# The last stage of a hybrid encoder block: the final norm's weights applied before the norm's power is known

## What is computed

```
u = causal_depthwise_conv(h @ w_up, ffn_conv_w) + ffn_conv_b
gate, val = jnp.split(u, 2, axis=-1)
y = (gelu(gate) * val) @ w_down
return x + rms_norm(y, g_post_ffn)     # y * rsqrt(mean(y*y) + EPS) * g_post_ffn
```

## Time and profile before

| | us |
|---|---|
| median of 3 runs | 1303.62 (1303.28 to 1305.38) |
| the profiled execution's own time | 1303.67 |
| its span in the profile | 1301.4 |
| TensorE (PE) busy | 1255.1 (96%) |
| VectorE (DVE) busy | 696.9 (54%) |
| ScalarE (ACT) busy | 410.7 (32%) |
| GpSimd (POOL) busy | 148.3 (11%) |

### The profile page before, as it was taken

The page is one execution under the profiler, slowest core; times in us unless marked ns, Lnnn a source line. Parts: engine busy times, 40 slices in busy tenths (PEclk is TensorE's granted clock), DMA queues, the critical chain, the costliest instruction groups (busy, mean ns, idle before and its releaser), DMA issues.

```text
span 1301.4 us, 17346 instructions
## 1 busy us (share of the span) xinstructions
PE 1255.1 (96%) x6360; PEld 1062.5 (82%) x6360; DVE 696.9 (54%) x1069; ACT 410.7 (32%) x754; POOL 148.3 (11%) x183
## 2 busy tenths in 40 slices
PE   6999999997999999899999999999999999999997
PEld 5888888876888889778888888888888888888875
DVE  6332454657767777563563636363636363535366
ACT  5121243645444444353312121212121212121321
POOL 1321001302322232121000000000000000000005
PEclk9999999997999999999999999999999999999999
DMA  8321233564233331232211111111111111110133
GB/s 275 123 80 54 81 103 103 150 190 121 73 110 109 108 108 45 92 106 81 78 52 46 50 44 53 41 55 39 58 36 60 34 62 34 62 34 30 37 125 129
DMA packets 90762, 106.52 MB, mean 82 GB/s; under 512 B 17471, under 2 KB 75615, under 8 KB 90719
## 3 DMA queue, kind: packets, MB, share of 16 engines
q1 hardware_dynamic: 90719, 105.96, 25.2%
HBM read 82.84 MB, written 23.10 MB: 81 GB/s over the span
## 4 chain that ended last, share of the span: by engine, by line
PE 53%; POOL 1%; issue 1%; DVE 0%; ACT 0%; POOLq 0%; DVEq 0%
PE f_ps_up L2383 12%; PE f_ps_up L2385 12%; PE f_ps_up L2384 12%; PE sums L2394 5%; PE sums L2395 5%; PE sums L2396 5%; POOL stage L2101 1%; POOL f_conv L2101 0%; POOL f_stat L2367 0%; POOLq L2006 0%; DVE split L2336 0%; DVE h_t L2301 0%; DVE f_conv L2101 0%; ACT x_tile L2233 0%; DVE h_t L2259 0%
## 5 line engine op out<-in xcount | busy, mean ns | idle before, releaser
L2383 PE MATMUL f_ps_up<-split,f_w_hi 128*128 128x512 f32 x704 | 274.3, 390 | 1.7 <-DVEq L2237 1.5
L2385 PE MATMUL f_ps_up<-split,f_w_lo 128*128 128x512 f32 x704 | 273.9, 389 | 0.0
L2384 PE MATMUL f_ps_up<-split,f_w_hi 128*128 128x512 f32 x704 | 273.9, 389 | 0.0
L2247 DVE SCALAR_TENSOR_TENSOR f_conv<-f_ps_up,f_taps,f_conv 128x1023 f32<-128x1023 f32 x88 | 112.8, 1282 | 272.3 <-ACT f_conv L2176 266.8
L2383 PEld LDWEIGHTS f_ps_up<-split,f_w_hi 128*128 128x128 f32 x704 | 132.1, 188 | 29.9 <-DVEq L2237 1.9
L2385 PEld LDWEIGHTS f_ps_up<-split,f_w_lo 128*128 128x128 f32 x704 | 132.1, 188 | 27.5
L2176 ACT ACTIVATE f_conv<-f_ps_up,f_taps 128x1024 f32<-128x1024 f32 x44 | 53.1, 1207 | 321.4 <-PE f_ps_up L2385 321.4
L2384 PEld LDWEIGHTS f_ps_up<-split,f_w_hi 128*128 128x128 f32 x704 | 132.2, 188 | 27.3
L2259 DVE TENSOR_TENSOR h_t<-sums,h_t 128x512 f32<-128x512 f32 x168 | 111.0, 685 | 39.9 <-PE sums L2396 39.7
L2394 PE MATMUL sums<-f_w_hi,f_y_hi 128*128 128x512 f32 x320 | 124.6, 389 | 0.0
L2396 PE MATMUL sums<-f_w_hi,y_lo 128*128 128x512 f32 x320 | 124.5, 389 | 0.0
(11 more groups left out here) (320 smaller groups left out, 2058.8 us busy)
## 6 DMA issues: line engine op xcount, KB each, us to landing
stage<-in_w_up SPq DMA_DIRECT2D x22, 1024.0 KB, 5.1
stage<-in_w_down SPq DMA_DIRECT2D x11, 1024.0 KB, 4.9
x_tile<-in_x SPq DMA_DIRECT2D x12, 512.0 KB, 4.0
stage<-in_w_in SPq DMA_DIRECT2D x6, 1024.0 KB, 6.7
qkv<-conv SPq DMA_DIRECT2D x11, 512.0 KB, 3.6
rows<-p_row SPq DMA_DIRECT2D x8, 644.0 KB, 3.2
stage<-rows SPq DMA_DIRECT2D x8, 644.0 KB, 4.0
res<-x_tile SPq DMA_DIRECT2D x8, 512.0 KB, 2.9
```

The source lines that it names most:

```text
L2247: op = dve.scalar_tensor_tensor(conv[:, q, k:S], ps_up[:, q % 2, 0:S - k], taps[:, bass.ds(ct + (FTAPS - 1 - k) * 2 * FT, 1)], conv[:, q, ...
L2383: pe.matmul(bank, hi, h_hi[:, k, cols], start=(k == ends[0]), stop=False)
L2384: pe.matmul(bank, hi, h_lo[:, k, cols], start=False, stop=False)
L2385: op = pe.matmul(bank, lo, h_hi[:, k, cols], start=False, stop=(k == ends[1]))
```

## The change

Four edits, all in the last stage.

- The square of a row tile is made in two halves of 512 columns, each as soon as its half is accumulated; the two sums go to two columns of `f_stat`.
- The mean is made in two steps on VectorE: `mean` takes the first half's sum, `mean_late` adds the second half's.
- The weights are multiplied in by two operations of 128 x 512, from `acc` into a separate tile `scaled` that lies where `raw_rest` and the start of `split` lie, before the power is known. `finish` then is one operation over 128 x 1024, on VectorE: `scaled` by the row's number, plus the residual.
- GpSimd makes the powers only. VectorE's order for a row tile now is: accumulate the first half, scale it, `mean`; accumulate the second half, scale it, `mean_late`, `finish` of the same row tile; then the next row tile.

```diff
-            eng.tensor_tensor(res_tile(t), res_tile(t), acc[:, t], ALU.add).then_inc(s_res, 1)
+        self.late = under("late", [P, D])
+        scaled = kept.late
@@ scalar
-                act.wait_ge(s_acc, LAST_SUM + 2 * t + 2 + 4)
-                act.activation(junk[:], acc[:, t], ACT.Square, accum_out=stat[:, 0, t:t + 1]).then_inc(s_sq, 1)
+                for half in range(2):
+                    cols = slice(half * HALF, (half + 1) * HALF)
+                    act.wait_ge(s_acc, LAST_SUM + 2 * t + half + 1 + 4)
+                    act.activation(junk[:, cols], acc[:, t, cols], ACT.Square, accum_out=stat[:, SUMS + half, t:t + 1]).then_inc(s_sq, 1)
@@ vector
+            def scale(t, half):
+                cols = slice(half * HALF, (half + 1) * HALF)
+                dve.wait_ge(s_acc, LAST_SUM + 2 * t + half + 1 + 4)
+                if t >= 1:
+                    dve.wait_ge(s_res, t)
+                dve.tensor_tensor(scaled[:, cols], acc[:, t, cols], gain[:, cols], ALU.mult).then_inc(s_norm, 1)
+            def mean(t):
+                dve.wait_ge(s_sq, 2 * t + 1)
+                dve.tensor_scalar(stat[:, MEAN, t:t + 1], stat[:, SUMS, t:t + 1], 1.0 / D, EPS, ALU.mult, ALU.add).then_inc(s_ms, 1)
+            def mean_late(t):
+                dve.wait_ge(s_sq, 2 * t + 2)
+                dve.wait_ge(s_ms, 2 * t + 1)
+                dve.scalar_tensor_tensor(stat[:, MEAN, t:t + 1], stat[:, SUM_LATE, t:t + 1], 1.0 / D, stat[:, MEAN, t:t + 1],
+                                         ALU.mult, ALU.add).then_inc(s_ms, 1)
             def finish(t):
-                if t == T - 1:
-                    residual(dve, t - 1)
                 dve.wait_ge(s_rstd, t + 1)
-                dve.scalar_tensor_tensor(acc[:, t], acc[:, t], stat[:, 2, t:t + 1], gain[:], ALU.mult, ALU.mult).then_inc(s_norm, 1)
-                if t == T - 1:
-                    residual(dve, t)
+                dve.wait_ge(s_norm, 2 * t + 2)
+                dve.wait_ge(s_xr[t // 4], 64)
+                dve.scalar_tensor_tensor(res_tile(t), scaled[:], stat[:, RSTD, t:t + 1], res_tile(t), ALU.mult, ALU.add).then_inc(s_res, 1)
-            for t in range(T + 1):
-                if t < T:
-                    for half in range(2):
-                        accumulate(LAST_SUM + 2 * t + half, t, half)
-                if t >= 1:
-                    finish(t - 1)
-                if t < T:
-                    dve.wait_ge(s_sq, t + 1)
-                    dve.tensor_scalar(stat[:, 1, t:t + 1], stat[:, 0, t:t + 1], 1.0 / D, EPS, ALU.mult, ALU.add).then_inc(s_ms, 1)
+            for t in range(T):
+                accumulate(LAST_SUM + 2 * t, t, 0)
+                scale(t, 0)
+                mean(t)
+                accumulate(LAST_SUM + 2 * t + 1, t, 1)
+                scale(t, 1)
+                mean_late(t)
+                finish(t)
@@ gpsimd
-                pool.wait_ge(s_ms, t + 1)
-                pool.tensor_tensor(stat[:, 2, t:t + 1], stat[:, 1, t:t + 1], power[:], ALU.pow).then_inc(s_rstd, 1)
-                if 1 <= t < T - 1:
-                    residual(pool, t - 1)
+                pool.wait_ge(s_ms, 2 * t + 2)
+                pool.tensor_tensor(stat[:, RSTD, t:t + 1], stat[:, MEAN, t:t + 1], power[:], ALU.pow).then_inc(s_rstd, 1)
```

More of the change, by code:

```diff
@@ L2025, in ffn_block @@
         taps = sb("f_taps", [P, NT + 2 * FT])
-        stat = sb("f_stat", [P, 3, T])
+        stat = sb("f_stat", [P, 5, T])
         power = sb("f_power", [P, 1])
@@ L2094, in res_tile @@
             return raw[:, 1 - t // 2, t % 2 * D:(t % 2 + 1) * D] if t < 4 else conv[:, t - 4]
[L2096 to L2100, removed]
-            eng.tensor_tensor(res_tile(t), res_tile(t), acc[:, t], ALU.add).then_inc(s_res, 1)
+        SUMS, SUM_LATE, MEAN, RSTD = 0, 1, 2, 3
+        scaled = kept.late
         @block.sync
```

## The result

| | before | after |
|---|---|---|
| median in us (22 runs each, taken side by side) | 1304.45 | 1306.39 |
| the profiled execution's own time | 1303.67 | 1306.49 |
| its span | 1301.4 | 1304.7 |
| first accumulation of the last stage to VectorE's last end ("the stretch") | 1260.96 to 1298.39: 37.43 | 1261.32 to 1301.67: 40.35 |

The ratio of the times, after over before, is 1.0015, 95% interval 1.0009 to 1.0022: 1.9 us slower, between 1.2 and 2.9. A second series (11 runs of the changed kernel, in the experiments) gives 1.0024, 1.0012 to 1.0036. Slower is settled; on which side of 0.2% it lies isn't. The stretch is the better ruler, since it holds all that the change touches: 2.92 us longer.

What follows compares the result with a forecast made beforehand. TensorE was taken to set the pace, with a 6.22 us tail behind it. Changed, eight VectorE turns of 5.07 us plus 0.08 end at 1301.60, not 1298.39: 1303.67 + 3.2 = 1306.9 us, range 1305.0 to 1309.0.

Steps and rivals of the forecast that it cites:

- late mean behind the first accumulation's start: In VectorE's turn: `mean_late` starts 3.03 us after the turn's first accumulation starts, behind the second half's square.
- finish, likewise: In VectorE's turn: `finish` starts 3.87 us after the first accumulation starts, after a stall on GpSimd's power.
- a turn: VectorE's sequence for one row tile, first accumulation to the next tile's: 5.07 us, run eight times.
- tail from the last accumulation: After the last sum: accumulation, half square, mean, power and finish take 3.59 to 3.60 us in place of 6.22.
- TensorE's wait ahead of sum 8: In the last stage, sum 8 waits for accumulation 4 on VectorE, losing TensorE 1.4 us.
- TensorE's end ahead of VectorE's last accumulation: TensorE ends at about 1293.6, 4.4 us before VectorE asks for sum 15; this is TensorE's slack.
- the unknown prices: Operations without their own row: square of 512 columns, taken as 0.63 us, and the power, taken as 0.55.
- the same mechanism, smaller terms: Rival: VectorE's turn is between 4.34 and 4.99 us, so the loss is under 0.2%; about 1306; chance 0.2.
- The rival of the other side: VectorE keeps up with a turn of at most 4.24 us, only the tail counts; time 1301.05; chance 0.04.
- Longer turns: Rival: VectorE's joined operations don't overlap and the power is 0.67; turn 5.35 us, time 1309.1; chance 0.06.
- the lost clock: Rival: TensorE drops to 1.2 GHz in the wait ahead of sum 8; time 1324; chance 0.01.
- several waits cost nothing: Several waits ahead of one VectorE operation add nothing that shows; tile 7's residual starts 0.03 us behind its last.

Runs made afterwards that it cites:

- after_fewer_mm: The changed kernel with sums 8 to 15 of the last stage made of 6 matmuls in place of 12; stretch 40.34 us.
- power_twice: The changed kernel with a second power on GpSimd ahead of each real one; stretch 44.39 us, ratio to the kernel before 1.0077.
- lag: The changed kernel with finish(t-1) moved behind the first accumulation of tile t; stretch 35.57 us, median 1302.82, ratio to the kernel before 0.9979.
- lag_whole: As lag, with whole square, scaling and mean for tiles 0 to 6, halves for tile 7; stretch 34.79 us, ratio to the kernel before 0.9980.
- square_whole: The changed kernel with one whole square and one mean per row tile, scaling still by halves; stretch 42.02 us, ratio to the kernel before 1.0024.
- lag_swap: As lag, with the two waits ahead of the scaling in the other order; stretch 35.08 us after 35.57.
- mean_behind: The changed kernel with the first half's mean moved behind the second half's scaling; stretch 39.54 us, ratio to the kernel before 1.0010.

## Why the prediction was right, point by point

| step of the prediction | forecast, us | measured, us |
|---|---|---|
| second accumulation behind the first | 1.55 | 1.55 |
| late mean behind the first accumulation's start | 3.03 | 3.02 |
| finish, likewise | 3.87 | 3.84 |
| a turn | 5.07 | 5.03 |
| tail from the last accumulation | 3.60 | 3.56 |
| TensorE's wait ahead of sum 8 | 1.4 | 1.40 |
| TensorE's end ahead of VectorE's last accumulation | 4.4 | 3.9 |
| the stretch | 40.64 | 40.35 |
| change of the profiled execution | +3.2 | +2.8 |
| time | 1306.9 | 1306.39 (median) |

**The mechanism** is the one forecast: in-order issue puts the norm of tile t ahead of the accumulation of tile t + 1, and 5.03 us, eight times, are more than TensorE needs, which is 31.21 us to the last accumulation with 3.56 of tail behind it. after_fewer_mm shows that the length of TensorE's late sums has no part in it, power_twice that each turn counts in full, lag that the stall on the power is most of it (4.8 of the 5.6 us that the stretch is above those 34.8). Of the unknown prices, the square of 512 columns took 0.63 as in the row it was read from, and the power 0.54 every time.

**The size** is 0.3 us too large in the stretch. It comes from the turn: the late mean starts at 3.02 and not 3.03, the power takes 0.54 and not 0.55, and the sum's 3.86 was carried on as 3.87. That makes 0.03 at the finish and about 0.25 over eight turns. TensorE's slack was 0.5 us smaller than worked out: VectorE arrives 0.25 earlier for the reason just given; the matmuls right behind TensorE's wait were 0.34, 0.24 and 0.24 us apart and not 0.227, about 0.2 in all; and the forecast left out that the last matmul, at 0.39, is longer than their distance. It decided nothing. TensorE's last matmul ahead of its wait and the first two behind it:

```profile
1270.35 0.39 PE L2407 MATMUL sums<-f_w_hi,f_w_lo 128*128 128x512 f32 x1
1272.14 0.50 PE L2405 MATMUL sums<-f_w_hi,f_y_hi 128*128 128x512 f32 x1 [1.40 <-DVE h_t L2258]
1272.48 0.40 PE L2406 MATMUL sums<-f_w_lo,f_y_hi 128*128 128x512 f32 x1
```

The time of 1306.9 came out nearer than the loss did, and that is luck. The forecast loss was 3.2 us, the medians differ by 1.9; but it was added to a time before of 1303.67, and the median before is 1304.45 over 22 runs.

**The chances.** 0.76 lay on slower by over 0.2%, 0.2 on less than that. The trace gives 2.9 us, just over 0.2%; the 22 runs give 1.9, just under, with an interval over both. The rival "the same mechanism, smaller terms" isn't excluded by them as a description of the median. The prediction said itself that 0.08 a turn would decide it, and half of that was off. It also put 2.6 us as the least that a measurement can tell from no change; 22 runs told 1.9.

**The rival of the other side**, VectorE keeping up, was right about the tail and wrong about the turn: lag_whole, which meets the condition of 4.24 us a turn by its order (3.92), has the stretch it asked for (34.81 by its sum, 34.79 measured). The page of the Trainium skill weighed in the prediction ("VectorE: DVE Perf Modes", section "Rules for kernel authors") advises to minimize the count of chained Vector operations, not of semaphores. Here the count didn't decide: with fewer operations the stretch was 1.7 us longer (square_whole), with the same ones in another order 4.8 shorter (lag). Both differences are waits for other engines, of which that rule says nothing. **Longer turns** and **the lost clock** didn't occur: operations overlap by 0.08 as before, and TensorE's granted clock reads 1.00 in both stretches shown above, the first of which holds its 1.4 us wait.

## What to carry to other kernels

On an engine that issues in order, look for something independent to stand between the links of a chain through other engines: one accumulation there took the 0.66 us stall away in lag. Shortening the last chain by moving its operations together puts the same waits into every turn before it. So lay out one turn with its waits, compare it with the pace of whoever feeds it, early tiles and late ones by themselves, and ask whether the engine still arrives in time for the last tile. Here the answer is to keep the lag of one tile through the loop and take the short form for the last tile alone.

## What the runs showed that was not expected

**The order of waits.** With two waits ahead of a VectorE operation, one met long ago and one met last, the operation starts 0.03 to 0.04 us behind the operation it waits for if the late wait stands first, and 0.10 to 0.11 if it stands second (lag and lag_swap, seen in both directions). The prediction's statement that several waits cost nothing was read from an operation whose late wait stood first. In the changed kernel the late wait stands first too, ahead of every scaling, late mean and finish, so the statement held there, by luck.

**What goes with the spread between runs.** The last stage starts anywhere between 1259.2 and 1264.4 us in these traces, although the instructions ahead of it are the same. The stretch from 300 to 330 us, between two stages far ahead of the change, shows it. The rows are of mean_behind, the kernel before, the changed kernel and lag, with the last stage's start at 1259.20, 1260.96, 1261.32 and 1264.40 in the same order (clock last but two):

```profile
300.00:330.00 30.00, 20.37 (x132) 18.80 (x132) 23.59 (x48) 15.80 (x55) 10.29 (x13) 0.83 0.31 86
```
```profile
300.00:330.00 30.00, 21.81 (x127) 20.64 (x128) 22.01 (x43) 14.41 (x46) 10.29 (x13) 0.72 0.30 82
```
```profile
300.00:330.00 30.00, 21.04 (x135) 19.55 (x133) 23.59 (x45) 15.20 (x47) 10.30 (x13) 0.77 0.28 82
```
```profile
300.00:330.00 30.00, 19.52 (x108) 18.27 (x109) 22.37 (x42) 14.01 (x46) 10.30 (x13) 0.66 0.29 81
```

TensorE is granted less than its full clock (2.4 GHz) for part of that stretch, where it is busy 19.5 to 21.8 of 30 us; for the changed kernel and for lag the 50 us ahead show 0.97 as well, for the other two 1.00. The time spent at the lower level (1.2 GHz) differs from run to run, and with it all that follows. The other nine traces agree in the main, though the groups overlap: by the granted clock between 300 and 330 us, the last stage starts at 1259.20 and 1260.40 (0.83), 1259.39 to 1261.56 (0.77), 1260.96 to 1262.58 (0.72), 1264.20 and 1264.40 (0.66). That the two go together is seen and not tested. These 5.2 us are more than the change is worth, so the place where the last stage starts moves a single run's time by more than the change does.
